# State-space mixing on one core: rows and mask by one split product, two heads in the array's halves, the gate's projection moved into the loop

## The chip, the cores and the metric

The kernel runs on one core of a Trainium2 chip. The metric is the device time of one execution in microseconds (us); lower is better. Before the change it is 3113.84 us, the median of three runs (3113.70 to 3118.78).

## The reference, cut to what matters

Two stacks of transformer-like blocks work on 256 tokens of width 1024, all in fp32. One layer of the second stack mixes the tokens with a two-way state-space scan, and the change is in that layer alone:

```python
z, xs, Bm, Cm, dt = project(u)      # one product with w_in; conv and silu on xs, Bm, Cm; softplus on dt
for d in range(2):                  # forward, and backward in time; 32 heads of 64, 4 groups, state 128
    a_cum = cumsum(dt * A)
    y_diag = (C B^T * exp(a_cum[l] - a_cum[s]) masked to s <= l) @ (x * dt[s])
    y_off  = exp(a_cum) * (C @ h_in)            # h_in: the state that the context left
    y += y_diag + y_off
y += d_skip * x
gy = y * silu(z)                    # z: 2048 columns of the same projection
out = (rmsnorm over each of 4 groups of 512 columns of gy) @ w_out
```

## The kernel before, in words

The whole program is a list of stages. Each of the five engines walks the list with its own function for each stage, in a fixed order, and semaphores alone join them. Names below are those of TensorE (PE), VectorE (DVE), ScalarE (ACT), GpSimd (POOL) and SyncE (SP).

**Weights** come as one stream of 852 units of 128 x 1024 values (512 KB) in the order of use. SP loads unit s into one of 8 slots as soon as unit s - 8 has been used (L549). ACT rounds it to fp32r (`split_hi`, L523), DVE takes the rest (`split_lo`, L536), and PE makes three passes over each of its 8 tiles (`three_pass`, L568 to L570): 24 matmuls of 256 columns a unit.

**The three stages around the change** are `ssd_in`, `mix` and `ssd_out`.

`ssd_in` projects and convolves x, B and C, and makes two tables with one row for each of 64 pairs of head and direction: `soft` (the step dt) and `rows` (its running sum times A). Its last steps are a chain between ACT (L2102 to L2111) and DVE (L2150 to L2163).

`mix` first turns the 16 tiles of x on PE (L2177), which ACT copies out (L2302), turns the rows into columns (`scols`, L2257, L2329) and makes the four products C B^T (L2263, copied by L2307). Then a loop runs over 64 items, each a head h and a direction d (i = 2h + d):

- PE copies row i of the running sum over all 128 partitions with an fp32 product with a column of the identity (L2278).
- DVE subtracts the column of the other token and adds the mask, 256 and 128 columns (L2341); ACT takes the exponential of the 384 (L2310); DVE multiplies it by the step's column and by C B^T (L2352).
- ACT also takes the exponential of the row itself (L2313), and POOL multiplies C by it (`c_exp`, L2322).
- PE adds up the item's output for 64 channels: x against the 384 columns (L2291), the state against `c_exp` (L2293). These products fill one half of the array's 128 columns; the half is h % 2. An fp32 product is two records in the trace.

Up to four items are in flight. Every fourth item closes a tile of 128 channels, which DVE adds to the skip term (`sy_out`, L2366).

`ssd_out` then runs over 16 gate units: PE projects z (24 matmuls), ACT applies Silu from PSUM (L2420), DVE multiplies (L2446), POOL squares (L2438), and PE adds the squares over the partitions (`sz_sum`, L2409). After the last one come the mean and the root (L2448, L2450, L2422), the rows of 1/length (L2391), the scaling and splitting of the 16 tiles (L2459, L2425, L2455) and the product with w_out: 16 units more.

What sets the order on PE in the loop, from `mix_tensor`: row i, then the products of item i - 3:

```python
for i in range(n + 3):
    if i < n:
        if i >= 4:
            pe.wait_ge(p.sem["g_exp"], a("g_exp") + i - 3)
        mm(p.psum[:, i % 4, 0:T], ident[0:ROWS, r : r + 1].to_broadcast([ROWS, P]), p.rows[0:ROWS],
        ...
    if i >= 3:
        ...
        pe.wait_ge(p.sem["sw_ready"], a("sw_ready") + k + 1)
        pe.wait_ge(p.sem["c_dec"], a("c_dec") + k + 1)
```

## Time and profile before

| | |
|---|---|
| median of 3 runs | 3113.84 us |
| the profiled execution | 3113.68 us, span 3111.8 us |
| busy in the span | PE 95%, DVE 74%, ACT 45%, POOL 12% |
| mean granted TensorE clock | 0.973 |
| setup of `mix` (turns, columns, C B^T) | 2240.8 to 2254.7 us |
| loop of `mix`, 64 items | 2254.7 to 2373.6 us |
| 16 gate units in `ssd_out` | 2374.1 to 2429.0 us |

The profile is one execution. Times in it are counted from the first instruction. The sum of the prediction is made against the profiled execution's own time, which is 1.9 us above its span and 0.16 us under the median. The granted clock is a share of 2.4 GHz; 0.5 is 1.2 GHz.

### The profile page before, as it was taken

To read this page: it belongs to the slowest core of one execution; us is meant where nothing else is said; L and a number is where in the kernel's file an instruction comes from. 1 tells how busy PE (TensorE), PEld (TensorE's weight loads), DVE (VectorE), ACT (ScalarE), POOL (GpSimd) and SP (SyncE) were. 2 spreads that over 40 slices of the span, in tenths; PEclk is the share of its full clock that TensorE was granted. 3 is DMA by queue.
4 is the path that set the end of the run, shared out by engine and by line. 5 is a ranking of instruction groups with operands and counts; after the bars stand their busy time and mean duration, and the time that the engine had idled before them with its cause. 6 is when DMAs were issued, how large, how long until landed. Compare 5 with 4: busy or idle time off the path is not lost.

```text
span 3111.8 us, 61666 instructions
## 1 busy us (share of the span) xinstructions
PE 2944.5 (95%) x24640; PEld 2780.6 (89%) x24640; DVE 2304.5 (74%) x3787; ACT 1395.5 (45%) x2211; POOL 380.9 (12%) x418
## 2 busy tenths in 40 slices
PE   5999999999999999999999997899899999999898
PEld 5999887899999988789999997799856899999798
DVE  7999565578878865556887888688886679777654
ACT  3446443444444553454444446444644444443342
POOL 0025011010201200101010030002042100102002
PEclk9999999999999999999999998999999899999899
DMA  9994303468878541225887873587402478776353
GB/s 343 348 366 157 111 15 102 136 212 328 299 264 283 191 135 36 80 97 183 309 321 259 307 265 122 183 313 257 140 1 68 136 277 325 243 260 233 102 189 129
DMA packets 172724, 632.15 MB, mean 203 GB/s; under 512 B 19168, under 2 KB 19552, under 8 KB 172000
## 3 DMA queue, kind: packets, MB, share of 16 engines
q1 hardware_dynamic: 123696, 450.75, 40.5%
q10 hardware_dynamic: 48816, 178.41, 16.3%
q8 instruction: 153, 2.51, 0.3%
q14 instruction: 59, 0.48, 0.0%
HBM read 628.04 MB, written 1.05 MB: 202 GB/s over the span
## 4 chain that ended last, share of the span: by engine, by line
PE 86%; DVE 10%; ACT 3%; issue 1%; DMA 1%; DVEq 0%; ACTq 0%; POOL 0%; SPq 0%
PE psum L568 23%; PE psum L570 23%; PE psum L569 23%; DVE w_lo L536 2%; DVE xl L2136 2%; PE psum L2291 2%; PE psum L586 1%; PE psum L2278 1%; PE psum L587 1%; PE psum L2293 1%; DVE bc L2136 1%; PE psum L592 1%; PE psum L1482 1%; PE psum L1485 1%; PE psum L2199 1%
## 5 line engine op out<-in xcount | busy, mean ns | idle before, releaser
L568 PE MATMUL psum<-h_hi,w_hi 128*128 128x256 f32 x4464 | 1256.6, 282 | 1.8 <-ACT qn L1927 0.9
L569 PE MATMUL psum<-h_hi,w_lo 128*128 128x256 f32 x4464 | 1249.7, 280 | 0.0
L570 PE MATMUL psum<-h_lo,w_hi 128*128 128x256 f32 x4464 | 1249.1, 280 | 0.0
L536 DVE TENSOR_TENSOR w_lo<-raw,w_hi 128x1024 fp32r<-128x1024 f32 x852 | 1067.9, 1256 | 202.7 <-ACT w_hi L523 201.7
L523 ACT ACTIVATE w_hi<-raw 128x1024 fp32r<-128x1024 f32 x852 | 874.6, 1054 | 391.7 <-DMA raw<-stream_dram 248.9
L568 PEld LDWEIGHTS psum<-h_hi,w_hi 128*128 128x128 f32 x4464 | 843.0, 189 | 14.9 <-issue 5.7
L569 PEld LDWEIGHTS psum<-h_hi,w_lo 128*128 128x128 f32 x4464 | 843.0, 189 | 0.5
L570 PEld LDWEIGHTS psum<-h_lo,w_hi 128*128 128x128 f32 x4464 | 842.9, 189 | 0.0
L568 PE MATMUL psum<-u_hi,w_hi 128*128 128x256 f32 x1584 | 441.9, 279 | 0.0
L569 PE MATMUL psum<-u_hi,w_lo 128*128 128x256 f32 x1584 | 441.9, 279 | 0.0
L570 PE MATMUL psum<-u_lo,w_hi 128*128 128x256 f32 x1584 | 441.9, 279 | 0.0
L615 DVE CUSTOM_DVE_ANT_0 ada_w<-ada_w,tmp 128x1024 f32<-128x1024 f32 x312 | 386.6, 1252 | 4.4 <-ACT tmp L623 4.4
L880 ACT ACTIVATE gate<-psum 128x256 f32<-128x256 f32 x198 | 76.2, 385 | 576.3 <-PE psum L570 565.8
L709 POOL TENSOR_TENSOR tmp<-x 128x256 f32<-128x256 f32 x91 | 110.6, 1218 | 1714.4 <-DVE x L930 1320.0
L570 PEld LDWEIGHTS psum<-u_lo,w_hi 128*128 128x128 f32 x1584 | 297.7, 188 | 0.0
L568 PEld LDWEIGHTS psum<-u_hi,w_hi 128*128 128x128 f32 x1584 | 297.7, 188 | 0.0
L569 PEld LDWEIGHTS psum<-u_hi,w_lo 128*128 128x128 f32 x1584 | 297.7, 188 | 0.0
L907 DVE TENSOR_TENSOR mid<-gate,psum 128x256 f32<-128x256 f32 x198 | 83.5, 422 | 198.7 <-ACT gate L880 198.7
L713 POOL TENSOR_TENSOR tmp<-tmp 128x256 f32<-128x256 f32 x78 | 93.7, 1201 | 6.1
L586 PE MATMUL psum<-h_hi,w_hi 128*128 128x256 f32 x208 | 73.2, 369 | 21.1 <-ACT h_hi L774 21.1
L1105 DVE SCALAR_TENSOR_TENSOR qkv<-conv_in,par,qkv 128x256 f32<-128x256 f32 x144 | 81.5, 567 | 12.2 <-ACT conv_in L1029 8.8
L915 DVE TENSOR_TENSOR u_lo<-mid,u_hi 128x256 fp32r<-128x256 f32 x198 | 84.2, 425 | 6.8
...
## 6 DMA issues: line engine op xcount, KB each, us to landing
raw<-stream_dram SPq DMA_DIRECT2D x852, 512.0 KB, 4.2
...
```

Source lines behind the costliest of these rows:

```text
L523: p.nc.scalar.activation(p.w_hi[:, slot].rearrange("p k m -> p (k m)"), p.raw[:, slot], ACT.Copy).then_inc(p.sem["hi_ready"], 1)
L536: p.nc.vector.tensor_tensor(p.w_lo[:, slot].rearrange("p k m -> p (k m)"), p.raw[:, slot], p.w_hi[:, slot].rearrange("p k m -> p (k m)").b ...
L568: mm(out, p.w_hi[:, slot, k], hi, start=start, stop=False, skip_group_check=skip)
L569: mm(out, p.w_lo[:, slot, k], hi, start=False, stop=False, skip_group_check=skip)
L570: return mm(out, p.w_hi[:, slot, k], lo, start=False, stop=stop, skip_group_check=skip)
L586: mm(out, p.w_hi[:, slot, k], p.h_hi[:, k], start=start, stop=False, skip_group_check=True)
L615: p.nc.vector.tensor_tensor_reduce(p.ada_w[:, slot], p.ada_w[:, slot], row, 1.0, 0.0, ALU.mult, ALU.add, p.ada_raw[:, s : s + 1]).then_inc ...
L709: p.nc.gpsimd.tensor_tensor(to, x[:, m], x[:, m], mult).then_inc(p.sem["sq_ready"], 1)
L713: p.nc.gpsimd.tensor_tensor(p.sq_sum, p.sq_sum, to, ALU.add).then_inc(p.sem["sq_ready"], 1)
L907: nc.vector.tensor_tensor(p.mid[:, t % 2], p.gate[:, t % 2], p.psum[:, t % 2, T : 2 * T], ALU.mult).then_inc(p.sem["mid_step"], 1)
L915: nc.vector.tensor_tensor(p.u_lo[:, t], p.mid[:, t % 2], p.u_hi[:, t].bitcast(F32), ALU.subtract).then_inc(p.sem["mid_ready"], 1)
L2136: v.scalar_tensor_tensor(out, src[:, j : j + T], w[:, t, j : j + 1], out, ALU.mult, ALU.add).then_inc(p.sem["conv_step" if i < 3 else "con ...
```

## The change

It touches the end of `ssd_in`, `mix`, and the start of `ssd_out`. Nothing else in the program moves; the stream of weights has the same order.

- **Rows and mask by TensorE.** The running sums are split into two fp32r parts, stacked on 128 partitions (`row_parts`). For an item PE makes one fp32r product of 512 columns with a 0/1 column repeated 128 times (`pick_r`): the row, twice side by side in a whole PSUM bank. A second fp32r product of 256 columns with the identity adds the mask (`neg_r`) to two of the four quarters.
- **Column and step as bias.** The column now holds ln(dt) minus the running sum. ACT's exponential reads PSUM and takes this column as its bias: two instructions for 256 and 128 columns. DVE keeps one multiplication of 384 columns by C B^T (stored in the order in which both directions can read 384 columns in a row). Both of DVE's L2341 and L2352 are gone. For the logarithm `ssd_in` has one more DVE and one more ACT instruction, and for the split rows one more of each, and one more DVE instruction for the new column.
- **Items in pairs.** Step q handles the heads h and h + 1 of one direction. Their products alternate between the two halves of the array, and each product of 256 columns by `sw` is now two of 128: 2 x 256 columns for the state, 6 x 128 for x. The products of q follow two steps after its rows. The ring of `sw` has 6 places instead of 4, that of `c_exp` 4 instead of 3.
- **Gate units in the loop.** Every second step, after the rows and ahead of the products, PE projects one of the 16 tiles of z, with its weights split by ACT and DVE in the same step. Silu(z) becomes z (1 + tanh(z/2)), with the factor of one half left to the norm: ACT makes Tanh, DVE one instruction (`gate`), and `out` adds the skip term and multiplies at once.
- **Squares.** POOL squares the gated tiles in the loop and adds four of a group, so that PE sums 4 tiles at the end instead of 16.

The diff, with the old bodies of the loops left out, since they stand above:

```diff
+SH = 32
+ROWS = 2 * SH
+N_X, N_BC = 16, 4
+SW_RING = 6
+Z_BANKS = (4, 7)
+TINY = 1.0e-30
...
-UNITS = {"ffn": 2 * FT + FT, "project": 39, "up": 10, "attn": KD, "gates": 32, "ssd_out": 32, "pool": 2}
+UNITS = {"ffn": 2 * FT + FT, "project": 39, "up": 10, "attn": KD, "gates": 32, "mix": N_X, "ssd_out": N_X, "pool": 2}
...
+        self.unit_r = self.over("unit_r", 0, [P, P + ROWS], F32R)
+        self.ident_r, self.pick_r = self.unit_r[:, 0:P], self.unit_r[:, P : P + ROWS]
...
-        self.cbt = self.over("cbt", 32768, [P, 4, 2, T])
+        self.cbt = self.over("cbt", 32768, [P, 4, 4 * P])
-        self.c_exp = self.over("c_exp", 71680, [P, 3, T])
-        self.sw = self.over("sw", 65536, [P, 4, 3 * P])
+        self.c_exp = self.tmp[:, 0:4]
+        self.sz_sums = self.tmp[:, 4:8]
+        self.sz_part = self.sin[:]
+        self.sw = self.over("sw", 65536, [P, SW_RING, 3 * P])
+        self.z_gate = (self.var, self.rinv)
...
+    else:
+        act.wait_ge(p.sem["dt_step"], a("dt_step") + 3)
+        f(p.sin[0:ROWS], p.sin[0:ROWS], ACT.Ln).then_inc(p.sem["gate_fn"], 1)
+        act.wait_ge(p.sem["dt_step"], a("dt_step") + 7)
+        f(p.row_parts[0:ROWS], p.rows[0:ROWS], ACT.Copy).then_inc(p.sem["gate_fn"], 1)
...
+    if not st.on_ctx:
+        link(v.tensor_scalar(p.sin[0:ROWS], dt, TINY, None, ALU.max))
...
-        v.tensor_tensor(p.rows[bwd], e[bwd], p.rinv[bwd], ALU.add).then_inc(p.sem["dt_ready"], 1)
+        link(v.tensor_tensor(p.rows[bwd], e[bwd], p.rinv[bwd], ALU.add))
+        dve.wait_ge(p.sem["gate_fn"], a("gate_fn") + 6)
+        v.tensor_tensor(p.row_parts[ROWS : 2 * ROWS], rows, p.row_parts[0:ROWS].bitcast(F32), ALU.subtract).then_inc(p.sem["dt_ready"], 1)
+        v.tensor_tensor(p.soft[0:ROWS], p.sin[0:ROWS], rows, ALU.subtract).then_inc(p.sem["dt_ready"], 1)
...
...
+    for c in range(2):
+        ins = mm(p.psum[:, 4, c * ROWS : c * ROWS + ROWS], p.soft[0:ROWS, c * P : c * P + P], ident[0:ROWS, 0:ROWS],
+                 start=True, stop=True)
...
+    pe.wait_ge(p.sem["tables_rounded"], a("tables_rounded") + 3)
+    def row(i):
+        h, d = item(i)
+        r = d * SH + h
+        if i >= 4:
+            pe.wait_ge(p.sem["sx_exp"], a("sx_exp") + i - 3)
+        mm(p.psum[:, i % 4], p.pick_r[:, r : r + 1].to_broadcast([P, P]),
+           p.row_parts[:].unsqueeze(1).broadcast_to([P, 2, T]), start=True, stop=False)
+        mask = p.neg_r[:, d]
+        mm(p.psum[:, i % 4, T * (1 - d) : T * (1 - d) + T], p.ident_r,
+           mask.unsqueeze(1).broadcast_to([P, 2, P]), start=False, stop=True).then_inc(p.sem["g_row"], 1)
+    def z_unit(t):
+        if t >= 2:
+            pe.wait_ge(p.sem["sz_made"], a("sz_made") + t - 1)
+        pe.wait_ge(p.sem["lo_ready"], u0 + t + 1)
+        for k in range(UNIT):
+            ins = three_pass(p, p.psum[:, Z_BANKS[t % 2], 0:T], (u0 + t) % SLOTS, k, p.h_hi[:, k], p.h_lo[:, k],
+                             k == 0, k == UNIT - 1)
+        ins.then_inc(p.sem["unit_done"], 1)
+    def products(q):
+        h, d = item(2 * q)
+        bank = 5 + q // 2 % 2
+        if d == 0 and q >= 4:
+            pe.wait_ge(p.sem["sy_out"], a("sy_out") + q // 2 - 1)
+        pe.wait_ge(p.sem["c_dec"], a("c_dec") + 2 * q + 2)
+        for e in range(2):
+            side, heads = slice(64 * e, 64 * e + 64), slice(64 * (h + e), 64 * (h + e) + 64)
+            mm(p.psum[side, bank, 0:T], p.state[:, d, heads], p.c_exp[:, (2 * q + e) % 4], start=d == 0, stop=False,
+               skip_group_check=True)
+        pe.wait_ge(p.sem["sw_ready"], a("sw_ready") + 2 * q + 2)
+        for n, s, to in SPANS[d]:
+            for e in range(2):
+                side, heads = slice(64 * e, 64 * e + 64), slice(64 * (h + e), 64 * (h + e) + 64)
+                ins = mm(p.psum[side, bank, to * P : to * P + P], p.x_tok[:, s, heads],
+                         p.sw[:, (2 * q + e) % SW_RING, n * P : n * P + P], start=False, stop=d == 1 and n > 0,
+                         skip_group_check=True)
+        ins.then_inc(p.sem["sy_part"], 1)
+    for q in range(SH + 2):
+        if q < SH:
+            row(2 * q)
+            row(2 * q + 1)
+            if q % 2:
+                z_unit(q // 2)
+        if q >= 2:
+            products(q - 2)
 def mix_scalar(p, act, st):
-    a, f = st.at, p.nc.scalar.activation
+    a, u0, f = st.at, st.unit0, p.nc.scalar.activation
+    f(p.ident_r, p.c("ident"), ACT.Copy).then_inc(p.sem["tables_rounded"], 1)
+    f(p.pick_r, p.c("pick2"), ACT.Copy).then_inc(p.sem["tables_rounded"], 1)
...
+    def tanh(t):
+        act.wait_ge(p.sem["unit_done"], u0 + t + 1)
+        if t >= 2:
+            act.wait_ge(p.sem["sz_gated"], a("sz_gated") + t - 1)
+        f(p.z_gate[t % 2][:], p.psum[:, Z_BANKS[t % 2], 0:T], ACT.Tanh, scale=0.5).then_inc(p.sem["gate_act"], 1)
+    act.wait_ge(p.sem["cols_ready"], a("cols_ready") + 1)
+    f(p.neg_r[:], p.c("neg").rearrange("p (d n) -> p d n", d=3)[:, 0:3:2], ACT.Copy).then_inc(
+        p.sem["tables_rounded"], 1)
+    for q in range(SH):
+        if q and q % 2 == 0:
+            tanh(q // 2 - 1)
+        for i in (2 * q, 2 * q + 1):
+            h, d = item(i)
+            act.wait_ge(p.sem["g_row"], a("g_row") + i + 1)
+            if i >= 4:
+                act.wait_ge(p.sem["c_dec"], a("c_dec") + i - 3)
+            f(p.g_exp[:, i % 4], p.psum[:, i % 4, T * d : T * d + T], ACT.Exp).then_inc(p.sem["g_exp"], 1)
+            if i >= SW_RING:
+                act.wait_ge(p.sem["sy_part"], a("sy_part") + (i - SW_RING) // 2 + 1)
+            at = (P, 3 * P, 4 * P) if d == 0 else (0, P, 3 * P)
+            for s in range(2):
+                ins = f(p.sw[:, i % SW_RING, at[s] - at[0] : at[s + 1] - at[0]], p.psum[:, i % 4, at[s] : at[s + 1]], ACT.Exp,
+                        bias=p.scols[:, 0, s, d * SH + h : d * SH + h + 1])
+            ins.then_inc(p.sem["sx_exp"], 1)
+        if q % 2:
+            split_hi(p, act, u0 + AHEAD + q // 2)
+    tanh(N_X - 1)
 def mix_gpsimd(p, pool, st):
...
+    a, tt = st.at, p.nc.gpsimd.tensor_tensor
+    def square(t):
+        g, n = t // 4, t % 4
+        pool.wait_ge(p.sem["sz_gated"], a("sz_gated") + t + 1)
+        if n == 0:
+            tt(p.sz_sums[:, g], p.sxbc(t), p.sxbc(t), ALU.mult).then_inc(p.sem["sz_sq"], 1)
+            return
+        if t > 1:
+            pool.wait_ge(p.sem["sz_added"], a("sz_added") + 3 * g + n - 1)
+        tt(p.sz_part, p.sxbc(t), p.sxbc(t), ALU.mult).then_inc(p.sem["sz_sq"], 1)
+        pool.wait_ge(p.sem["sz_sq"], a("sz_sq") + t + 1)
+        tt(p.sz_sums[:, g], p.sz_sums[:, g], p.sz_part, ALU.add).then_inc(p.sem["sz_added"], 1)
+    pool.wait_ge(p.sem["cols_ready"], a("cols_ready") + 1)
+    for q in range(SH):
+        for i in (2 * q, 2 * q + 1):
+            pool.wait_ge(p.sem["g_exp"], a("g_exp") + i + 1)
+            if q >= 2:
+                pool.wait_ge(p.sem["sy_part"], a("sy_part") + q - 1)
+            tt(p.c_exp[:, i % 4], p.sxbc(N_X + N_BC + i // 16), p.g_exp[:, i % 4], ALU.mult).then_inc(p.sem["c_dec"], 1)
+        if q >= 5 and q % 2:
+            square((q - 5) // 2)
+    square(N_X - 2)
+    square(N_X - 1)
...
+    def gate(t):
+        z = p.z_gate[t % 2][:]
+        dve.wait_ge(p.sem["gate_act"], a("gate_act") + t + 1)
+        v.scalar_tensor_tensor(z, z, 1.0, p.psum[:, Z_BANKS[t % 2], 0:T], ALU.add, ALU.mult).then_inc(p.sem["sz_made"], 1)
+    def out(j):
+        dve.wait_ge(p.sem["sy_part"], a("sy_part") + 2 * j + 2)
+        v.scalar_tensor_tensor(
+            p.sxbc(j), p.sxbc(j), st.par(p, "d_skip")[:, j : j + 1], p.psum[:, 5 + j % 2, 0:T], ALU.mult, ALU.add
+        ).then_inc(p.sem["sy_out"], 1)
+        dve.wait_ge(p.sem["sy_out"], a("sy_out") + j + 1)
+        dve.wait_ge(p.sem["sz_made"], a("sz_made") + j + 1)
+        v.tensor_tensor(p.sxbc(j), p.sxbc(j), p.z_gate[j % 2][:], ALU.mult).then_inc(p.sem["sz_gated"], 1)
+    for q in range(SH):
+        for i in (2 * q, 2 * q + 1):
+            h, d = item(i)
+            dve.wait_ge(p.sem["sx_exp"], a("sx_exp") + i + 1)
+            part = p.sw[:, i % SW_RING]
+            v.tensor_tensor(part, part, p.cbt[:, h // 8, P * d : P * d + 3 * P], ALU.mult).then_inc(p.sem["sw_ready"], 1)
+        if q % 2:
+            split_lo(p, dve, u0 + AHEAD + q // 2)
+        elif q:
+            gate(q // 2 - 1)
+            if q >= 4:
+                out(q // 2 - 2)
+    gate(N_X - 1)
+    out(N_X - 2)
+    out(N_X - 1)
...
 def ssd_out_tensor(p, pe, st):
     a, u0, mm = st.at, st.unit0, p.nc.tensor.matmul
     pe.wait_ge(p.sem["sy_out"], a("sy_out"))
...
+    for g in range(4):
+        pe.wait_ge(p.sem["sz_added"], a("sz_added") - 9 + 3 * g)
+        ins = mm(p.psum[0:16, 6, 0:T], p.pick("row", g), p.sz_sums[:, g], start=g == 0, stop=g == 3)
+    ins.then_inc(p.sem["sz_summed"], 1)
     pe.wait_ge(p.sem["o_root"], a("o_root") + 1)
```

What the order of the instructions is on PE in the middle of the loop. Before, two items:

```order
L2278 MATMUL psum<-rows,const 128x256
L2291 MATMUL psum<-sw,x_tok 64x256
L2291 MATMUL psum<-sw,x_tok 64x128
L2293 MATMUL psum<-c_exp,state 64x256
L2278 MATMUL psum<-rows,const 128x256
L2291 MATMUL psum<-sw,x_tok 64x256
L2291 MATMUL psum<-sw,x_tok 64x128
L2293 MATMUL psum<-c_exp,state 64x256
```

Each row is followed by the two kinds of products of one item. After, one step without a gate unit and the start of one with it (`tmp` is `c_exp`; L581 to L583 are `three_pass`, and there are eight such triples a unit):

```order
L2299 MATMUL psum<-row_parts,unit_r 128x512
L2302 MATMUL psum<-neg_r,unit_r 128x256
L2299 MATMUL psum<-row_parts,unit_r 128x512
L2302 MATMUL psum<-neg_r,unit_r 128x256
L2322 MATMUL psum<-tmp,state 64x256 x2
L2328 MATMUL psum<-sw,x_tok 64x128 x6
L2299 MATMUL psum<-row_parts,unit_r 128x512
L2302 MATMUL psum<-neg_r,unit_r 128x256
L2299 MATMUL psum<-row_parts,unit_r 128x512
L2302 MATMUL psum<-neg_r,unit_r 128x256
L581 MATMUL psum<-h_hi,w_hi 128x256
L582 MATMUL psum<-h_hi,w_lo 128x256
```

The rows of two items stand together, then the products of two items, whose eight instructions go to alternate halves of the array.

On ACT at the end of `ssd_in` and the start of `mix`. Before:

```order
L2111 ACT_TABLE_LOAD
L2111 ACTIVATE var<-var 64x256
L2302 ACTIVATE x_tok<-psum 128x256 x16
L2307 ACTIVATE cbt<-psum 128x512 x4
L2310 ACT_TABLE_LOAD
```

The copies of x follow the last logarithm at once. After, on the same engine and place:

```order
L2121 ACT_TABLE_LOAD
L2121 ACTIVATE var<-var 64x256
L2127 ACTIVATE sin<-sin 64x256
L2129 ACTIVATE row_parts<-rows 64x256
L2345 ACTIVATE unit_r<-const 128x128
L2346 ACTIVATE unit_r<-const 128x64
L2350 ACTIVATE x_tok<-psum 128x256 x16
L2355 ACTIVATE cbt<-psum 128x512 x4
L2364 ACTIVATE neg_r<-const 128x256
L2374 ACT_TABLE_LOAD
```

Four instructions now stand ahead of the copies of x, two of which wait for DVE's tables, and one behind those of C B^T. Inside the loop, ACT loads no table.

On DVE in the middle of the loop, one pair of items before (a tile is closed in every second pair):

```order
L2341 SCALAR_TENSOR_TENSOR sw<-psum,scols,const 128x256
L2341 SCALAR_TENSOR_TENSOR sw<-psum,scols,const 128x128
L2352 SCALAR_TENSOR_TENSOR sw<-sw,scols,cbt 128x256
L2352 SCALAR_TENSOR_TENSOR sw<-sw,scols,cbt 128x128
L2341 SCALAR_TENSOR_TENSOR sw<-psum,scols,const 128x256
L2341 SCALAR_TENSOR_TENSOR sw<-psum,scols,const 128x128
L2352 SCALAR_TENSOR_TENSOR sw<-sw,scols,cbt 128x256
L2352 SCALAR_TENSOR_TENSOR sw<-sw,scols,cbt 128x128
```

Four instructions for each item, in two kinds that took turns. After, on the same engine, two steps with one gate unit:

```order
L2441 TENSOR_TENSOR sw<-sw,cbt 128x384 x2
L549 TENSOR_TENSOR w_lo<-raw,w_hi 128x1024
L2441 TENSOR_TENSOR sw<-sw,cbt 128x384 x2
L2425 SCALAR_TENSOR_TENSOR var<-var,psum 128x256
L2429 SCALAR_TENSOR_TENSOR xl<-xl,par,psum 128x256
L2434 TENSOR_TENSOR xl<-xl,rinv 128x256
```

The eight instructions of a pair became two; one weight split, one gate, one skip term and one product with the gate came in for every two pairs.

## Rows read from the trace of the kernel before

**Rows 1.** The page: the chain that ended last, by engine.

```profile
PE 86%; DVE 10%; ACT 3%; issue 1%; DMA 1%; DVEq 0%; ACTq 0%; POOL 0%; SPq 0%
```

**Rows 2.** Stretches: us, each engine's busy us (instructions), granted clock, DMA.

```profile
core 0: us, PE busy (x) PEld busy (x) DVE busy (x) ACT busy (x) POOL busy (x), PEclk, DMA share, GB/s
2245.30:2249.10 3.80, 3.71 (x17) 3.38 (x17) 2.12 (x5) 3.42 (x13) 0.00 (x0) 0.50 0.02 4
2249.30:2254.70 5.40, 4.68 (x24) 3.61 (x24) 0.42 (x1) 2.92 (x7) 0.00 (x0) 1.00 0.00 0
2254.70:2373.60 118.90, 117.18 (x512) 62.55 (x512) 96.30 (x272) 54.27 (x131) 46.60 (x64) 1.00 0.00 1
2373.60:2429.00 55.40, 54.87 (x411) 47.41 (x412) 26.79 (x32) 20.04 (x31) 9.24 (x15) 1.00 0.42 143
```

**Rows 3.** Timeline of one loop item on PE: start us, us, engine, line.

```profile
2335.24 0.69 PE L2278 MATMUL psum<-rows,const 64*128 64x256 f32 x2
...
2335.86 0.86 PE L2291 MATMUL psum<-sw,x_tok 128*64 128x256 f32 x4
...
2336.56 0.59 PE L2293 MATMUL psum<-c_exp,state 128*64 128x256 f32 x2
...
2337.09 0.69 PE L2278 MATMUL psum<-rows,const 64*128 64x256 f32 x2
```

**Rows 4.** Timeline of PE at the loop's end, where no rows stand between.

```profile
2370.31 0.87 PE L2291 MATMUL psum<-sw,x_tok 128*64 128x256 f32 x5
2370.96 0.38 PE L2293 MATMUL psum<-c_exp,state 128*64 128x256 f32 x1
2371.01 0.38 PE L2291 MATMUL psum<-sw,x_tok 128*64 128x256 f32 x1
2371.18 0.38 PE L2293 MATMUL psum<-c_exp,state 128*64 128x256 f32 x1
...
2371.45 0.59 PE L2293 MATMUL psum<-c_exp,state 128*64 128x256 f32 x2
```

**Rows 5.** Timeline of PE: 24 matmuls apart in the first gate units.

```profile
2374.47 0.28 PE L570 MATMUL psum<-h_lo,w_hi 128*128 128x256 f32 x1
...
2377.27 0.28 PE L570 MATMUL psum<-h_lo,w_hi 128*128 128x256 f32 x1
```

**Rows 6.** Groups, 2249 to 2432 us: line, engine, op, shapes, count, busy us, mean ns.

```profile
L2322 POOL TENSOR_TENSOR c_exp<-bc,g_exp 128x256 f32<-128x256 f32 x64 | 46.6, 729 | 168.4 <-ACT g_exp L2313 168.4
L2313 ACT ACTIVATE g_exp<-psum 128x256 f32<-128x256 f32 x64 | 23.4, 366 | 0.0
L2438 POOL TENSOR_TENSOR tmp<-xl 128x256 f32<-128x256 f32 x16 | 9.9, 616 | 49.0 <-DVE xl L2446 49.0
L2366 DVE SCALAR_TENSOR_TENSOR xl<-xl,par,psum 128x256 f32<-128x256 f32 x16 | 7.6, 475 | 1.4 <-PE psum L2293 1.4
L2446 DVE TENSOR_TENSOR xl<-xl,sz 128x256 f32<-128x256 f32 x16 | 6.8, 426 | 21.1 <-ACT sz L2420 21.1
L2307 ACT ACTIVATE cbt<-psum 128x512 f32<-128x512 f32 x4 | 2.4, 597 | 2.5 <-PE psum L2263 2.5
```

**Rows 7.** The page: groups of the weights' split.

```profile
L536 DVE TENSOR_TENSOR w_lo<-raw,w_hi 128x1024 fp32r<-128x1024 f32 x852 | 1067.9, 1256 | 202.7 <-ACT w_hi L523 201.7
L523 ACT ACTIVATE w_hi<-raw 128x1024 fp32r<-128x1024 f32 x852 | 874.6, 1054 | 391.7 <-DMA raw<-stream_dram 248.9
```

**Rows 8.** Timeline of the end of `ssd_in` and the setup of `mix`.

```profile
2244.71 3.35 ACT L2302 ACTIVATE x_tok<-psum 128x256 f32<-128x256 f32 x12
...
2245.39 3.68 PE L2177 MATMUL psum<-const,xl 128*128 128x128 f32 x16 [0.90 <-ACT x_tok L2302]
...
2247.15 0.41 DVE L2163 TENSOR_TENSOR rows<-var,rinv 32x256 f32<-32x256 f32 x1
```

**Rows 9.** Chain that ended last, behind the last gate unit: start us, us, what.

```profile
2428.94 0.39 ACT sz L2420
...
2431.17 0.42 DVE soft L2448
```

**Rows 10.** One line of POOL over the whole program: duration ns min/median/max.

```profile
L713 POOL TENSOR_TENSOR tmp<-tmp x78: 731/1596/1682, 190.6 to 3096.9; 128x256 f32<-128x256 f32 x78
```

166 lines of the change are left out of this document (29 added, 137 removed).

## Prediction

> **What bounds the kernel now.** I read the page's chain first, then the stretches, then single items. The chain that ended last is 86% PE [rows 1]. In the loop of `mix` PE is busy 117.18 of 118.90 us at a full granted clock, DVE 96.30, ACT 54.27, POOL 46.60; in the stretch of the 16 gate units PE is busy 54.87 of 55.40 us [rows 2]. So both stretches are PE's, and the change is worth what it takes from PE, as long as the others stay under the new pace.
>
> One loop item shows how PE spends its time. Rows start at 2335.24 and again at 2337.09 us, so an item takes 1.853 us (118.6 us / 64) [rows 3]. Inside it the products by `sw` start 0.62 us after the row, those by the state 0.70 us later, the next row 0.53 us later. At the loop's end four records by `sw` (256, 256, 128, 128 columns) start with 2370.31 and are followed by the two by the state at 2370.96 and 2371.18 [rows 4]: 0.65 us for 768 columns and 0.22 for 256, so 0.108 us for each 128 columns of a record. All six take 1.08 us, and the row's two records of 256 columns 0.43, 1.51 us in all. The other 0.34 us of an item are spent at the two changes of shape, from 64 x 128 to 128 x 64 and back. In a gate unit 24 fp32r matmuls of 256 columns take 2.80 us, 0.117 each [rows 5].
>
> **Part 1, the setup.** ACT's copies of x start at 2244.71, and PE's second batch of turns waits for the first of them until 2245.39 [rows 8]. Now ACT first waits for DVE's last table. That one ended at 2247.56 [rows 8]; one DVE instruction more ahead of it (0.4) makes 2247.95, then ACT rounds the rows (0.4, from the 0.366 of a copy of this width [rows 6]) and copies two small tables (0.5): the copies of x start at about 2248.9, 4.2 us later. DVE's two further instructions lie beside this. `neg_r` adds 0.4 us behind the last copy of C B^T. PE idles 5 us instead of 0.9. Its clock is 0.50 in the second batch and 1.00 from 2249.3 on, when PE had been back at work for about 4 us [rows 2]; after the longer rest it should come back about 4 us after 2249.6, near the end of the turns. I take 0.9 us for that. Sum **+5.5 us**; bounds 4.6 (clock back at once) and 8.4 (all 3.8 us of C B^T at half the clock).
>
> **Part 2, the loop.** Two steps are four items and one gate unit. On PE:
> - Rows: four products of 512 fp32r columns and four of 256. No row shows 512 columns. From below 0.213 us (one column per cycle of 2.4 GHz; the same gives 0.107 for 256, where [rows 5] have 0.117), from above twice 0.117; I take 0.223, as the 0.01 on top is paid once. With 0.117 for the mask: 4 x 0.34 = 1.36 us.
> - Gate unit: 2.80 us [rows 5], same shape as the rows, so no change between them.
> - Products: in one half 2 x 0.216 for the state and 6 x 0.108 for x, 1.08 us. The other half's stand beside them, if halves overlap. The end of the loop shows it: the last records by the state of one item start at 2370.96 and 2371.18, and records by `sw` of the next, in the other half, at 2371.01 and between them [rows 4]. Two items of 1.08 us end at 2371.45 + 0.43, 1.57 us after 2370.31, not 2.16 later. Two steps: 2.16 us.
> - Changes of shape: 2 x 0.34 = 0.68 us.
> - Alternation: the new order changes half at each product; before only once. The first record after the switch was followed by the next 0.05 us later than within a run. Bounds 0 and 0.20 a step (four in each half, 0.05 each); I take 0.10, so 0.20 for two steps.
>
> Sum 7.20 us, sixteen times: **115.2 us** for all 32 pairs and all 16 gate units.
>
> The Trainium skill, "TensorE: Matmul & The Clock Gate", Part 3 on packing small matmuls, says that matmuls start and end strictly in program order. The rows speak against it: the record of 2371.01 stands behind that of 2371.18 in the program. By that rule the second record of one half and the first of the other would share a slot, and a step would cost one slot of 0.11 to 0.22 us more than full overlap, which would make the sum 115 to 119 us.
>
> Do the others keep pace with 7.20 us? ACT: for each item 256 columns from PSUM (0.366), another 256 and 128; from 256 and 512 columns (0.366, 0.597) I estimate 0.25 for 128: 3.9 us for four items, plus one weight split 1.05 and Tanh about as `g_exp`: 5.4 us [rows 6, 7]. Were a bias to cost 0.05 more in each, 5.8. DVE: 384 columns lie between 256 (0.426) and 1024 (1.256), about 0.56, four of them 2.2; split 1.26, gate and skip 0.48 each, product 0.43: 4.6 us [rows 6, 7]. POOL: 4 x 0.73, a square 0.62, and in three of four an addition 0.62: 4.0 us [rows 6]. All lie under 7.20. In latency the loop is loose too: an item's rows are used two steps later, with a gate unit always in between, so from rows to products there are over 5 us for ACT (1.0), DVE (0.6) and POOL (0.7). Rows wait for the exponential four items back. The weights come at one unit in 7.2 us, where before it was one in 3.5. The removed DVE instructions (96 us busy) give nothing, since PE set the pace.
>
> **Part 3, the end.** From the last gate unit's Silu at 2428.94 to L2448 at 2431.17 it took 2.4 us, counted from the last matmul [rows 9]. Now the last products are followed by skip term and gate product on DVE (0.95 us), square and addition on POOL (1.3) and the last sum on PE: 3.3 us. The 14 sums that stood between gate units, some 0.65 us each with their changes of shape (3.45 a unit against 2.80), are gone from PE; they are in the stretch replaced. The rest of `ssd_out` is as it was.
>
> **Sum.** Before, from the first row at 2254.7 to L2448 at 2431.2: 176.5 us. After: 5.5 + 115.2 + 3.3 = 124.0. Gain 52.5 us; 3113.7 - 52.5 = **3061 us**. The profiled execution is 0.2 us from the median, so the same against it. Faster means by more than 0.2%, 6.2 us, about what a measurement can tell.
>
> **Rivals.**
>
> *A. The halves do not overlap when they alternate after every product.* For it: before, only one switch at a time is seen, and PE would have to look past the second record of one product. Against: in [rows 4] it did run more than one record ahead. Each step then costs 1.08 us more: 32 x 1.08 = 34.6, 3096 us.
>
> *B. POOL and DVE get in each other's way.* One and the same POOL instruction takes 731 ns at best and 1596 in the median [rows 10], and `c_exp` takes 0.73 where a square takes 0.62 [rows 6]. If POOL stood still whenever DVE reads two SBUF tensors (4 x 0.56 + 1.26 + 0.43 = 3.9 us), both together need 4.0 + 3.9 = 7.9 us for two steps: 0.7 x 16 = 11 us more, 3072 us. Before, POOL had 1.1 us to spare in an item of 1.85; now little is left if this holds. The Trainium skill, "SBUF — State Buffer", section on two separate sides, has this as a rule: the pair of ports that both share is locked for a whole instruction.
>
> *C. Slower than before.* Each change of half costs like half of a change of shape (0.17 us) and nothing overlaps. A step has seven such changes: 1.08 + 7 x 0.17 - 0.10 = 2.2 us more, 32 times: 69 us, 3130 us. Without overlap the change loses from about 0.1 us a switch on (the gain of 52.5 / 32 = 1.64 us a step, less 0.98, by seven). For it: changes of shape do cost 0.34 an item. Against: the switch in [rows 4] cost 0.05 us in its own half and nothing in the other.
>
> *D. The loop does better:* alternation costs nothing and the clock is back at once: 3.2 + 0.9 us less, 3057 us; part of the forecast's own range.
>
> **Chances.** Forecast with D 0.70 (3052 to 3068), B or another engine's latency 0.13 (3068 to 3085), A 0.11, C 0.04, a loop better than my rows allow 0.02. The range 3051 to 3092 leaves out C, most of A and the last. Faster 0.95, same 0.01, slower 0.04.
>
> **What would show it.** In the loop's stretch PE busy near all the time, a gate unit every 7.2 us; records of both halves starting within 0.1 us of each other, eight products in about 1.1 to 1.3 us. Copies of x starting 4.2 us later behind the last logarithm. PE not waiting for POOL or ACT. I am wrong if two steps take over 7.6 us: if then the products take 2.1 us it is A, if PE waits for `c_exp` it is B. A pace under 6.9 us would mean that changes of shape cost less than I read.

## The result and the profile after

| us | before | changed | |
|---|---|---|---|
| median of 4 runs | 3113.77 (3112.64 to 3118.78) | 3062.09 (3059.13 to 3070.21) | ratio 0.9835, 95% interval 0.9814 to 0.9857 |
| profiled execution, its span | 3113.68, 3111.8 | 3061.89, 3060.1 | -51.7 (span) |
| first turn of x on PE | 2240.85 | 2243.78 | +2.9, upstream of every changed line |
| first turn to first row | 13.86 | 17.58 | +3.7 |
| first row to the start of the last product or z matmul | 173.9 | 113.1 | -60.8 |
| from there to the mean on DVE | 2.5 | 4.2 | +1.6 |
| the mean to the end | 680.6 | 681.5 | +0.9 |

The forecast was 3061 us, range 3051 to 3092, with 0.95 on faster. The time came out 1.1 us above the forecast.

One row of the table, the first turn, belongs to no edit: it moves by up to 11 us between the profiles below, of one and the same kernel too (2243.78 here, 2252.13 in a second profile of it). The clock stood at half for 114.3 us ahead of the first turn here and for 134.9 us in that second profile, but `fours` has its first turn at 2253.94 with 123.8 us, so the clock is at most a part of the cause. **The stretch** from the first turn to the mean is what the change touches, and it repeats: 134.83 us here, 134.81 in that second profile. It was 190.32 before. So the experiments are read by this stretch, and by the period, the time from one gate unit to the next in the loop.

The page's chain that ended last is still PE's:

```profile
PE 84%; DVE 11%; ACT 3%; issue 1%; DMA 1%; POOL 0%; DVEq 0%; ACTq 0%; POOLq 0%
```

Against [rows 1] PE has 2 points less, since all that was taken away was its own. The loop in windows, columns as in [rows 2], first the part at the low clock, then the part at the full clock, then ten periods of the loop:

```profile
core 0: us, PE busy (x) PEld busy (x) DVE busy (x) ACT busy (x) POOL busy (x), PEclk, DMA share, GB/s
2238.70:2255.70 17.00, 7.16 (x32) 6.55 (x32) 8.85 (x18) 11.29 (x29) 0.00 (x0) 0.50 0.01 2
2255.70:2382.00 126.30, 119.99 (x1072) 100.19 (x1072) 89.48 (x131) 88.12 (x235) 72.31 (x92) 1.00 0.20 68
2290.00:2360.00 70.00, 70.00 (x638) 58.59 (x637) 54.32 (x81) 50.98 (x139) 44.30 (x58) 1.00 0.23 76
```

PE is busy for all of 70 us; before, with the loop and the gate units apart, it was 117.18 of 118.90 and 54.87 of 55.40 [rows 2]. The records of DVE, ACT and POOL cover 54, 51 and 44 of 70 us, for ACT and POOL a larger share than in the loop of before. A record of DVE or POOL can hold a wait for the other; how near the two are to the bound is worked out under "The others' pace". The period is 7.067 us.

One period on PE, the 24 matmuls of the gate unit left out (they stand between 2303.80 and 2306.70):

```profile
2303.00 0.50 PE L2299 MATMUL psum<-row_parts,unit_r 128*128 128x512 f32 x1
2303.34 0.28 PE L2302 MATMUL psum<-neg_r,unit_r 128*128 128x256 f32 x1
2303.46 0.39 PE L2299 MATMUL psum<-row_parts,unit_r 128*128 128x512 f32 x1
2303.68 0.28 PE L2302 MATMUL psum<-neg_r,unit_r 128*128 128x256 f32 x1
...
2306.70 0.65 PE L2322 MATMUL psum<-tmp,state 128*64 128x256 f32 x4
2307.18 0.82 PE L2328 MATMUL psum<-sw,x_tok 128*64 128x128 f32 x12
2307.93 0.50 PE L2299 MATMUL psum<-row_parts,unit_r 128*128 128x512 f32 x1
...
2308.62 0.28 PE L2302 MATMUL psum<-neg_r,unit_r 128*128 128x256 f32 x1
2308.83 0.65 PE L2322 MATMUL psum<-tmp,state 128*64 128x256 f32 x4
```

A row of 512 columns lets its mask start 0.22 us later (2303.46 to 2303.68), the mask the next row 0.12 later; a row in all is 0.345 us, where [rows 3] had two records of 256 fp32 columns, 0.43. The sixteen records of a step, for both heads, take 1.23 us from 2306.70 to the next row at 2307.93. Before, one head's six took 1.08 and two heads' twelve 2.16 (a state product is still two records of 256 columns, and an x product of 128 columns two of 128). The changes of shape can be read too: 0.21 us from the last mask to the first state product (2308.62 to 2308.83) instead of 0.12; 1.23 for 1.08 of products; and the first row after them lasts 0.34 instead of 0.23. That is 0.09 + 0.15 + 0.11 = 0.35 us a step, as the 0.34 an item of before.

**Where the time came from.** PE's work in the loop and the gate units, before and after, worked out from these rows and [rows 3 to 5]:

| us on PE | before | after | gained |
|---|---|---|---|
| rows and mask | 64 x 0.432 = 27.6 | 64 x 0.345 = 22.1 | 5.5 |
| products of x and state | 64 x 1.08 = 69.1 | 32 x 1.08 = 34.6 | 34.5 |
| changes of shape | 64 x 0.34 = 21.8 | 32 x 0.35 = 11.2 | 10.6 |
| 16 gate units | 44.8 | 44.8 | 0 |
| 13 sums between gate units, 0.74 each | 9.6 | 0 | 9.6 |
| sum; measured | 172.9; 173.9 | 112.7; 113.1 | 60.2; 60.8 |

More than half of the gain is two heads side by side; half the changes of shape and the missing sums bring a third.

### The profile page after: what moved, and what is told of

The parts are those of the page before. It is cut to its first block, busy times and chain, and to the rows that moved or that the text cites. A ratio compares the mean times of both kernels' runs of the same rounds, so it can differ in the third digit from the quotient of the medians.

```text
span 3060.1 us, 61776 instructions
## 1 busy us (share of the span) xinstructions
PE 2890.5 (94%) x24756; PEld 2772.1 (91%) x24756; DVE 2267.7 (74%) x3614; ACT 1404.9 (46%) x2279; POOL 398.1 (13%) x430
## 3 DMA queue, kind: packets, MB, share of 16 engines
HBM read 628.07 MB, written 1.05 MB: 206 GB/s over the span
## 4 chain that ended last, share of the span: by engine, by line
PE 84%; DVE 11%; ACT 3%; issue 1%; DMA 1%; POOL 0%; DVEq 0%; ACTq 0%; POOLq 0%
PE psum L581 23%; PE psum L583 23%; PE psum L582 23%; DVE w_lo L549 3%; DVE xl L2151 2%; PE psum L599 1%; DVE ada_w L628 1%; PE psum L600 1%; DVE bc L2151 1%; PE psum L605 1%; PE psum L2299 1%; PE psum L1495 1%; PE psum L1498 1%; PE psum L2328 1%; PE psum L2219 1%
## 5 line engine op out<-in xcount | busy, mean ns | idle before, releaser
L581 PE MATMUL psum<-h_hi,w_hi 128*128 128x256 f32 x4464 | 1257.4, 282 | 1.2 <-ACT qn L1940 0.9
L583 PE MATMUL psum<-h_lo,w_hi 128*128 128x256 f32 x4464 | 1249.0, 280 | 0.0
L581 PEld LDWEIGHTS psum<-h_hi,w_hi 128*128 128x128 f32 x4464 | 843.1, 189 | 8.4 <-issue 5.3
L583 PEld LDWEIGHTS psum<-h_lo,w_hi 128*128 128x128 f32 x4464 | 843.0, 189 | 0.0
L581 PE MATMUL psum<-u_hi,w_hi 128*128 128x256 f32 x1584 | 442.8, 280 | 0.0
L583 PE MATMUL psum<-u_lo,w_hi 128*128 128x256 f32 x1584 | 442.0, 279 | 0.0
L583 PEld LDWEIGHTS psum<-u_lo,w_hi 128*128 128x128 f32 x1584 | 297.7, 188 | 0.0
L581 PEld LDWEIGHTS psum<-u_hi,w_hi 128*128 128x128 f32 x1584 | 297.6, 188 | 0.0
L1118 DVE SCALAR_TENSOR_TENSOR qkv<-conv_in,par,qkv 128x256 f32<-128x256 f32 x144 | 81.5, 567 | 12.7 <-ACT conv_in L1042 9.3
```

What stands on the lines that cost most here:

```text
L581: mm(out, p.w_hi[:, slot, k], hi, start=start, stop=False, skip_group_check=skip)
L583: return mm(out, p.w_hi[:, slot, k], lo, start=False, stop=stop, skip_group_check=skip)
```

## The experiments

Each is one edit of the changed kernel. The first four ran on one chip, one run each, beside 3119.01 us for the kernel before; the other four on a second chip, beside 3117.27 (9 runs). Where a time comes from one run, it is too coarse for a few us, and the stretch and the period decide. Line numbers in their rows are their own.

| | time us (runs) | stretch us | period us | POOL busy share in the loop |
|---|---|---|---|---|
| changed kernel | 3062.09 (4) | 134.83 | 7.067 | 0.63 |
| both heads in one half | 3096.76 (1) | 168.02 | 9.222 | 0.44 |
| one half after the other | 3081.26 (1) | 155.82 | 8.461 | 0.52 |
| gate units behind the loop | 3076.74 (1) | 136.05 | 4.256, no gate unit | 0.85 |
| POOL's multiplication twice | 3095.76 (1) | 165.56 | 9.069 | 0.99 |
| tables rounded during the turns | 3058.82 (4), ratio 0.9814 (0.9799 to 0.9829) | 133.22 | 7.067 | as changed |
| blocks of four rows | 3059.80 (4), ratio 0.9813 (0.9796 to 0.9830) | 131.41 | 6.718 | 0.85 |
| these two and a shorter tail | 3055.36 (5), ratio 0.9799 (0.9784 to 0.9813) | 127.46 | 6.718 | 0.85 |
| changed kernel again | 3062.89 (5), ratio 0.9830 (0.9813 to 0.9847) | 134.81 | 7.067 | 0.63 |

### Both heads in one half (`one_half`)

```diff
-            side, heads = slice(64 * e, 64 * e + 64), slice(64 * (h + e), 64 * (h + e) + 64)
+            side, heads = slice(0, 64), slice(64 * (h + e), 64 * (h + e) + 64)
```

(in both loops of the products; the channels of the odd heads are left out of the output)

> Both heads of a pair write the same half of the array's columns (channels of the odd head are left out of the output, everything else is as in the change). If the halves really overlap in the changed kernel, this takes the overlap away and nothing else: 1.08 us more for each of the 32 steps, two steps with a gate unit in 9.2 instead of 7.06 us, the whole 34 to 35 us slower than the change. If PE issues products one after the other anyway and the gain came from somewhere else, the pace stays at 7.06 us.

Measured: period 9.222 us, 2.156 more, 1.078 for each of two steps. Its timeline on PE, one step:

```profile
2305.18 1.08 PE L2322 MATMUL psum<-tmp,state 128*64 128x256 f32 x4
2306.10 1.47 PE L2328 MATMUL psum<-sw,x_tok 128*64 128x128 f32 x12
2307.50 0.50 PE L2299 MATMUL psum<-row_parts,unit_r 128*128 128x512 f32 x1
```

The same sixteen records take 2.32 us instead of 1.23. Rows, changes of shape and gate unit are as they were. So the overlap of the two halves hides one head's 1.08 us entirely, no more and no less, and the order of the products costs nothing beside it. Rival A would have looked like this profile; the changed kernel does not.

### One half after the other (`grouped`)

```diff
+        pe.wait_ge(p.sem["sw_ready"], a("sw_ready") + 2 * q + 2)
         for e in range(2):
             side, heads = ...
             mm(p.psum[side, bank, 0:T], p.state[:, d, heads], p.c_exp[:, (2 * q + e) % 4], ...)
-        pe.wait_ge(p.sem["sw_ready"], a("sw_ready") + 2 * q + 2)
-        for n, s, to in SPANS[d]:
-            for e in range(2):
+            for n, s, to in SPANS[d]:
                 ...
```

> The four products of one head, then the four of the other, in place of alternating after each product. If PE looks far enough ahead to start the other half's products from behind four products (16 records), nothing changes: 7.06 us for two steps. If it looks only a few records ahead, the second head starts late and a step costs up to 0.5 to 1.0 us more: 8 to 9 us for two steps, the whole 16 to 34 us slower than the change.

Measured: period 8.461 us, 0.70 a step more. One step of it on PE:

```profile
2304.98 0.65 PE L2323 MATMUL psum<-tmp,state 128*64 128x256 f32 x2
2305.46 0.49 PE L2326 MATMUL psum<-sw,x_tok 128*64 128x128 f32 x3
2305.68 0.43 PE L2323 MATMUL psum<-tmp,state 128*64 128x256 f32 x1
2305.79 0.38 PE L2326 MATMUL psum<-sw,x_tok 128*64 128x128 f32 x2
2305.95 0.38 PE L2323 MATMUL psum<-tmp,state 128*64 128x256 f32 x1
2306.01 0.98 PE L2326 MATMUL psum<-sw,x_tok 128*64 128x128 f32 x7
2306.91 0.50 PE L2299 MATMUL psum<-row_parts,unit_r 128*128 128x512 f32 x1
```

The first half's two state records and three x records run alone; the second half's first record starts at 2305.68, 0.70 us after the first. From then on both halves run beside each other, until the first has no more. The step takes 1.93 us, which is 1.23 + 0.70. So the order does matter, the other way round than I had feared: the alternation costs nothing, and its absence 0.70 us a step, 22 us in 32. PE reached the free half only when few records of the busy one were left: of the first half's eight, five had started by 2305.68 and three had not. Those three start at 2305.79, 2305.90 and 2306.01, behind a record that follows them in the program. It is so in every step of the loop, 0.71 us after the first record, whether the step stands behind a gate unit or behind rows alone. Whether this is how far PE looks ahead, or how fast it takes up instructions, was not separated.

### Gate units behind the loop (`gates_behind`)

```diff
         if q < SH:
             row(2 * q)
             row(2 * q + 1)
-            if q % 2:
-                z_unit(q // 2)
         if q >= 2:
             products(q - 2)
+    for t in range(N_X):
+        z_unit(t)
```

(and Tanh, splits, gate, product and squares behind the loops of the other engines)

> The 16 gate units stand behind the loop again, with Tanh, gate, product and squares; the loop is otherwise that of the change. PE has the same work, so if only PE's work counted the time would stay within 2 us of the change. My theory: a gate unit of 2.80 us in every second step is also the cover for ACT, DVE and POOL. Without it PE needs 4.26 us for two steps, but DVE four multiplications of up to 0.98 us and ACT four items of 0.9 us, so the pace should be 4.6 to 5.4 us instead of 4.26, and the whole 5 to 18 us slower than the change.

Measured: stretch 136.05 us, only 1.2 more than with the gate units in the loop; period 4.256, about 7.067 less a gate unit's 2.80. The first 50 us of the loop that are clear of the start, columns as above:

```profile
2280.00:2330.00 50.00, 49.93 (x472) 35.82 (x468) 44.37 (x62) 45.03 (x144) 42.52 (x48) 1.00 0.01 2
```

PE is busy 49.93 of 50 us though the records of DVE, ACT and POOL cover 85% to 90%. This speaks against a step of mine: I gave the gate unit's 2.80 us as what makes the latencies harmless. They are harmless without it, and what I expected of the bare loop was slower than it is. The expectation took the 0.98 us of a DVE multiplication for work, but more than half of that is a wait for POOL ("The others' pace" below): in turns, four multiplications on DVE and four on POOL need about 4 x (0.41 + 0.59) = 4.0 us, just under PE's 4.256. The time of this run, 3076.74, is not evidence against that: its first turn stands at 2253.62, 9.8 us later than in the changed kernel's profile, and its part behind the mean took 3.8 us more. This run has no sums between its gate units either, since POOL adds the squares here too. So the move into the loop by itself brought 1.2 us of the stretch; the 9.6 us of the sums come from POOL's additions and don't need the gate units in the loop.

### POOL's multiplication twice (`pool_double`)

```diff
+            if i >= 2:
+                pool.wait_ge(p.sem["c_dec"], a("c_dec") + i - 1)
+            tt(p.c("attn")[:, 0:T] if i % 2 else p.soft[:], p.sxbc(N_X + N_BC + i // 16), p.g_exp[:, i % 4], ALU.mult)
             tt(p.c_exp[:, i % 4], p.sxbc(N_X + N_BC + i // 16), p.g_exp[:, i % 4], ALU.mult).then_inc(...)
```

> POOL makes each product for c_exp twice, the first into an unused place. POOL's work for two steps rises from about 4.7 us (four of 0.85, a square and most of an addition) by 2.9 to 3.4 us to about 7.8 us. If POOL was near the bound, as the rival of GpSimd and VectorE says, the pace goes from 7.06 to 8 us or more: 15 us and more slower than the change. If POOL has the 2.4 us of slack that these numbers leave, the pace rises to about 7.8 only, 12 us slower; if DVE's reads no longer stretch POOL, it stays at 7.1.

Measured: period 9.069 us, 2.0 more. Windows of the same 70 us as above, POOL's timeline, and one record of DVE:

```profile
2290.00:2360.00 70.00, 58.16 (x501) 48.64 (x502) 52.40 (x64) 40.81 (x110) 69.53 (x76) 0.95 0.18 61
```

```profile
2300.25 1.05 POOL L2410 TENSOR_TENSOR soft<-bc,g_exp 128x256 f32<-128x256 f32 x1
2301.27 1.70 POOL L2411 TENSOR_TENSOR tmp<-bc,g_exp 128x256 f32<-128x256 f32 x1
2302.93 0.72 POOL L2410 TENSOR_TENSOR const<-bc,g_exp 128x256 f32<-128x256 f32 x1
2303.61 0.72 POOL L2411 TENSOR_TENSOR tmp<-bc,g_exp 128x256 f32<-128x256 f32 x1
...
2300.63 1.76 DVE L549 TENSOR_TENSOR w_lo<-raw,w_hi 128x1024 fp32r<-128x1024 f32 x1
```

POOL's records cover 69.53 of 70 us and PE has fallen to 58.16, at a mean granted clock of 0.95: this is how rival B looks when it decides. The same multiplication takes 0.72 us, 1.05 and once 1.70. Eight at 0.73 plus the square and the addition would be 7.2 us (8 x 0.73 + 0.62 + 0.75); the period is 9.07. The other 1.9 us are waits for DVE, as this split shows: it started at 2300.63 and ended at 2302.39, 1.08 us after POOL's first multiplication (2301.31); POOL's second started beside it at 2301.27 and ended at 2302.97, 0.58 us after the split.

### Tables rounded during the turns (`setup_early`)

```diff
-    f(p.ident_r, p.c("ident"), ACT.Copy).then_inc(p.sem["tables_rounded"], 1)
-    f(p.pick_r, p.c("pick2"), ACT.Copy).then_inc(p.sem["tables_rounded"], 1)
     for i in range(8):
+        if i == 4:
+            act.wait_ge(p.sem["dt_step"], a("dt_step") - 4)
+            f(p.sin[0:ROWS], p.sin[0:ROWS], ACT.Ln).then_inc(...)
+            act.wait_ge(p.sem["dt_step"], a("dt_step"))
+            f(p.row_parts[0:ROWS], p.rows[0:ROWS], ACT.Copy).then_inc(...)
+            f(p.ident_r, ...); f(p.pick_r, ...)
```

(the logarithm and the copy of the rows no longer stand ahead of the copies of x)

> ACT copies the first four groups of x before it waits for the tables of DVE; the logarithm, the rounded rows and the two small tables come behind them. Theory: in the change PE's second batch of turns starts 3.9 us late only because of this order. The stretch from the first turn to the first row should fall from 17.6 to 13.9 to 14.5 us, the whole 3 to 4 us faster than the change. Rival: the chain over DVE is needed for the columns anyway and the wait only moves there: 1 us or less.

Measured: from the first turn to the first row 15.97 us instead of 17.58, stretch 133.22. The median is 4.1 us under the changed kernel's on the same chip, of which this edit explains 1.6 in the one profile; the intervals of the two ratios overlap. PE's timeline, first of this kernel, then of the changed one:

```profile
2248.39 3.68 PE L2192 MATMUL psum<-const,xl 128*128 128x128 f32 x16 [0.89 <-ACT x_tok L2350]
2252.35 1.11 PE L2272 MATMUL psum<-const,soft 64*128 64x64 f32 x4 [0.29 <-DVE soft L2178]
2253.40 5.34 PE L2280 MATMUL psum<-bc 128*128 128x128 f32 x32
```

```profile
2252.19 3.68 PE L2197 MATMUL psum<-const,xl 128*128 128x128 f32 x16 [4.76 <-ACT x_tok L2350]
2256.38 3.90 PE L2285 MATMUL psum<-bc 128*128 128x128 f32 x32
...
2261.36 0.47 PE L2299 MATMUL psum<-row_parts,unit_r 128*128 128x512 f32 x1 [1.08 <-ACT neg_r L2364]
```

The wait of 4.76 us is gone and the turns start where they did before (0.89 of waiting, [rows 8] have 0.90). But more than half of the 3.86 us won there is given back: C B^T now takes 5.34 us instead of 3.90, the columns 1.11 instead of 0.66 and 0.29 of waiting for DVE before them, 2.2 us in all, because the clock is granted in full only from 2256.5 on, while in the changed kernel the late C B^T meets a clock that is already up (2255.7).

### Blocks of four rows (`fours`)

```diff
-    for q in range(SH + 2):
-        if q < SH:
-            row(2 * q)
-            row(2 * q + 1)
-            if q % 2:
-                z_unit(q // 2)
-        if q >= 2:
-            products(q - 2)
+    for m in range(N_X + 1):
+        if m < N_X:
+            for i in range(4 * m, 4 * m + 4):
+                row(i)
+            z_unit(m)
+        if m:
+            products(2 * m - 2)
+            products(2 * m - 1)
```

(with eight places for `sw` instead of six)

> Four rows, the gate unit, then the products of two steps: half as many changes of shape on PE (16 instead of 32 in and out), with 8 places for sw. Theory: a change in and out costs 0.35 us, so a gate unit's period falls from 7.06 to 6.71 us, 16 times: 5.6 us faster than the change. Rival: c_exp has only 4 places, and POOL can start on four items only when all products before them are done; POOL needs 3.4 to 3.8 us for them and the time until they are needed is 4.2 us: if it is late, the period stays at 7.0 or rises.

Measured: period 6.718 us, 0.349 less: one of two changes of shape in a period is gone, at the price read above. Sixteen times that is 5.6 us, but the loop is only 3.8 shorter (109.32 for 113.09), the stretch 3.4. The rest shows at the end of the loop, in the profile of the next kernel, which has the same loop:

```profile
2365.37 4.15 POOL L2419 TENSOR_TENSOR tmp<-bc,g_exp 128x256 f32<-128x256 f32 x4 [1.30 <-PE psum L2328]
...
2368.11 0.65 PE L2322 MATMUL psum<-tmp,state 128*64 128x256 f32 x4 [1.81 <-DVE xl L2440]
```

With nothing left but the last four items, PE waits 1.81 us. Two things end last and close together: POOL's second multiplication of the four, at 2367.96, since the whole four can start only when the products before have freed their places; and a skip term of DVE, at 2368.10, which stands behind a split of 1.75 us. Both are late by turns that the two engines take ("The others' pace" below): that multiplication took 1.70 us and the split 1.75, where alone they take 0.73 and 1.22. Which of the two alone would still hold PE wasn't separated.

### These two and a shorter tail (`all_three`)

```diff
+        if g == 3 and n:
+            ...
+            tt(p.sz_last[n - 1], p.sxbc(t), p.sxbc(t), ALU.mult).then_inc(p.sem["sz_sq"], 1)
+            return
```

(the last three squares are not added on POOL; PE sums them one by one, 7 products instead of 4)

> setup_early and fours together, and at the end POOL no longer adds the last three squares, PE sums them one by one (three additions of 0.73 us less behind the last products). Theory: 3.7 + 5.6 + 1.5 = 10.8 us faster than the change, about 3051 us. Rival: the period of fours is set by POOL, then 5 us.

Measured: 3055.36 us, ratio 0.9799 (0.9784 to 0.9813), the fastest of all kernels here; stretch 127.46, 7.4 less than the changed kernel, as much as the medians differ (3062.89 - 3055.36 = 7.5), where 10.8 were expected. From the first turn to the first row it takes 14.06 us; here the clock rose at 2255.7, in time for C B^T:

```profile
2256.31 3.90 PE L2285 MATMUL psum<-bc 128*128 128x128 f32 x32
```

so that 3.5 us were won where the edit alone won 1.6. It is the same edit, and up to there the same work; the clock rose 8.5 us after the first turn here and 12.7 there. That differs by execution, and with it this part. The tail edit gained 0.08 us of the 1.5 expected (4.09 for 4.17): PE's three products more take what POOL's additions took.

The single records at this kernel's last step are worth a look, since the two halves have different names there (the eighth place of `sw` lies in `const`):

```profile
2370.05 0.27 PE L2328 MATMUL psum<-sw,x_tok 128*64 128x128 f32 x1
...
2370.06 0.27 PE L2328 MATMUL psum<-const,x_tok 128*64 128x128 f32 x1
...
2370.16 0.27 PE L2328 MATMUL psum<-sw,x_tok 128*64 128x128 f32 x1
...
2370.17 0.27 PE L2328 MATMUL psum<-const,x_tok 128*64 128x128 f32 x1
```

A record of each half starts every 0.11 us, 0.01 us apart: two streams beside each other.

### The changed kernel again (`change_again`)

> The change itself once more on the same chip, to compare the others with: 3062 us, two steps with a gate unit in 7.06 us.

Measured: 3062.89 us, ratio 0.9830 (0.9813 to 0.9847), period 7.067, stretch 134.81. The first turn stood at 2252.13, 8.35 us later than in the first profile, and that execution took about as much longer (span 3068.3 for 3060.1). The stretch is the same within 0.02 us in the two profiles; what comes ahead of it is not.

## Why the prediction was right, and where it was off

**What bounds it.** PE before and after, shown by 70.00 busy of 70 us, and by `gates_behind` and `pool_double`: take work from PE and the pace falls to PE's; add work to POOL and PE waits.

**Part 1, the setup: 5.5 us forecast, 3.7 measured.** The copies of x started 7.72 us after the first turn instead of 3.86:

```profile
2250.84 0.42 ACT L2129 ACTIVATE row_parts<-rows 64x256 fp32r<-64x256 f32 x1 [1.51 <-DVE rows L2180]
...
2251.50 3.35 ACT L2350 ACTIVATE x_tok<-psum 128x256 f32<-128x256 f32 x12
```

That is 3.86 later against 4.2 forecast: rounding and the two small copies took 0.66 us, not 0.9. `neg_r` cost its 0.4. The 0.9 for the clock was not needed: it rose 3.5 us into the second batch of turns (0.50 until 2255.7, the batch 3.68 us as in [rows 8]), and C B^T ran at full speed. That the clock would be back about 4 us after PE was, the runs bear out only in part: from the start of the second batch to the rise it was 3.9 us before, 3.5 here and 4.0 in `all_three`, but 8.1 in `setup_early`. And I overlooked a gain: the four products that made columns of the running sum are gone, 0.6 us. 3.86 + 0.4 - 0.6 = 3.7. The bound from above, C B^T at half the clock, was no idle one: a good part of it is what `setup_early` ran into.

**Part 2, the loop: 7.20 us a period forecast, 7.07 measured; 115.2 and 113.1 in all.** Rows 1.36 against 1.38; gate unit 2.80; products 2.16; changes of shape 0.68 against 0.70. The alternation, for which I took 0.20, costs nothing, and that is nearly the whole difference: on this point rival D had it right. The steps that this rests on, that the halves overlap wholly and a change of shape costs 0.34, are each shown by an experiment that moves just that (1.078 and 0.349 us).

**The page's rule.** By records of one step that start in pairs 0.01 us apart, and by a period of 7.07, full overlap holds from the first record to the last. The rule of the Trainium skill that I weighed, "TensorE: Matmul & The Clock Gate", Part 3, strict program order of starts and ends, would have given 7.19 us or more by my working; the trace does not agree. `grouped` shows it for whole products too: the second half's state product starts at 2305.68, ahead of the first half's third x product at 2305.90, which stands before it in the program. Those who take the rule as a warning that order matters are right, though: that kernel lost 0.70 us a step by order alone.

**The others' pace.** I gave DVE 4.6 us a period (my own terms add up to 4.9); its records cover 5.5 (54.32 of 70). The 384-column multiplication takes 774 ns in the mean instead of 560. Two groups, 2244 to 2390 us of the changed kernel, columns as in [rows 6]:

```profile
L2408 POOL TENSOR_TENSOR tmp<-bc,g_exp 128x256 f32<-128x256 f32 x64 | 52.8, 845 | 144.9 <-ACT g_exp L2374 103.6 <-PE psum L2328 40.7
...
L2441 DVE TENSOR_TENSOR sw<-sw,cbt 128x384 f32<-128x384 f32 x64 | 47.6, 774 | 29.1 <-ACT sw L2379 28.9
```

POOL I gave 4.0; its records cover 4.5 (44.30 of 70), since `c_exp` went from 729 ns [rows 6] to 845. ACT: 5.2 by this window against 5.4 forecast. What DVE and POOL have more is waiting, not work. Five records in a row of the two engines, each from a window that holds it alone:

```profile
2309.55 0.61 POOL L2394 TENSOR_TENSOR tmp<-xl 128x256 f32<-128x256 f32 x1
2309.63 0.95 DVE L2441 TENSOR_TENSOR sw<-sw,cbt 128x384 f32<-128x384 f32 x1 [1.45 <-ACT sw L2379]
2310.29 0.89 POOL L2408 TENSOR_TENSOR tmp<-bc,g_exp 128x256 f32<-128x256 f32 x1
2310.52 1.07 DVE L2441 TENSOR_TENSOR sw<-sw,cbt 128x384 f32<-128x384 f32 x1
2311.14 1.05 POOL L2408 TENSOR_TENSOR tmp<-bc,g_exp 128x256 f32<-128x256 f32 x1
```

Each starts while the other engine's runs, and each ends the same time after the end of the one before it: DVE's multiplication 0.41 us (2310.58 after POOL's 2310.17, 2311.59 after 2311.18), POOL's 0.60 (2311.18 after 2310.58, 2312.19 after 2311.59). So it is in all 78 places of this loop where such records overlap by more than 0.06 us: 0.41 to 0.42 for DVE's multiplication, 0.59 to 0.60 for POOL's multiplication and addition, 0.28 to 0.29 for DVE's product with the gate. DVE's skip term, which reads PSUM and one tile of SBUF, takes 0.47 beside POOL and alone. In other words, where DVE reads two SBUF tensors, the two engines take turns for whole instructions, as rival B's condition says, and a record's length holds the wait. The records of the two cover 98.6 of 70 us because waits are in them.

What B had wrong was the sum: it added up full lengths, 7.9 us. In turns an instruction costs less, since part of its length passes beside the other's. From the times after the other's end, here and in `pool_double` (split 1.08, square 0.47), I estimate the shortest total for a period: 4 x 0.41 + 1.08 + 0.28 on DVE and 4 x 0.59 + 0.47 + 0.75 x 0.59 on POOL, 6.3 us. That is 0.8 under PE's 7.07, so the loop is nearer to this bound than the shares of busy time tell. With four multiplications more it is 8.6 at the shortest, and `pool_double` took 9.07.

**Part 3, the end: 3.3 us forecast, 4.2 measured.** The step that failed is that everything up to the last product would be in time, and that one square and one addition would follow it. POOL's and PE's timeline at the end:

```profile
2371.76 1.59 POOL L2408 TENSOR_TENSOR tmp<-bc,g_exp 128x256 f32<-128x256 f32 x2 [3.04 <-PE psum L2328]
2373.32 0.61 POOL L2398 TENSOR_TENSOR sin<-xl 128x256 f32<-128x256 f32 x1
2374.00 0.73 POOL L2400 TENSOR_TENSOR tmp<-tmp,sin 128x256 f32<-128x256 f32 x1
...
2377.19 0.72 POOL L2400 TENSOR_TENSOR tmp<-tmp,sin 128x256 f32<-128x256 f32 x1
```

```profile
2373.41 0.65 PE L2322 MATMUL psum<-tmp,state 128*64 128x256 f32 x4 [0.72 <-POOL tmp L2408]
...
2377.97 0.61 PE L2458 MATMUL psum<-tmp,const 128*16 128x256 f32 x2 [1.20 <-POOL tmp L2400]
```

The last pair's two multiplications come last of all and PE waits 0.72 us for them (this lies in the loop's 113.1). Behind them POOL has three squares and three additions in a row, not one of each, and is done at 2377.9; the last sum waits 1.20 us for it.

**Sum.** Stretch: 52.5 us forecast, 55.5 measured (1.8 in the setup, 2.1 in the loop, 0.9 lost at the end). The time then hit 1 us from the forecast because the first turn came 2.9 us later and the part behind the mean took 0.9 more, neither of them shown to be the change's doing (the part behind the mean took 680.7 to 683.9 us in the profiles of the experiments, `gates_behind` apart): the closeness is partly luck, and the gain itself was underrated by 3 us. One count in the prediction was off without entering the sum: 13 sums stood between gate units, not 14, and each cost 0.74 us (3.54 a unit), not 0.65.

What stays open: why the full clock came 8.5 us after the first turn in `all_three` and 12.7 in `setup_early`, with the same setup, which decides about 2 us; what sets the moment at which PE goes over to the free half; and whether the upstream differences have one cause.
